# A hybrid decoder trunk in fp32 on one core: which engine takes the low halves of the GLU weights, and which the convolution taps

## The chip, the cores and the metric

The kernel runs on one core of a Trainium2 chip. The metric is the device time of one execution in microseconds (us); lower is better.

## The reference

```python
def conv_recurrent_mixer(hn, w_in, conv_a_w, ...):
    u = hn @ w_in
    a_val, a_gate, xr, gr = jnp.split(u, [D_A, 2 * D_A, 2 * D_A + D_B], axis=-1)
    ya = a_val * jax.nn.sigmoid(a_gate)
    ya = causal_depthwise_conv(ya, conv_a_w, conv_a_b)      # 31 taps per channel
    ya = jax.nn.silu(layer_norm(ya, ln_a_g, ln_a_b))
    xr = causal_depthwise_conv(xr, conv_b_w, conv_b_b)      # 4 taps
    yb = rg_lru(xr, ...) * jax.nn.gelu(gr)
    return jnp.concatenate([ya, yb], axis=-1) @ w_out
```

Layer 0 runs this mixer, layer 1 a stick-breaking attention; each layer then has a squared-ReLU MLP and a gated per-layer embedding. D is 2048, the sequence has 256 tokens, D_A and D_B are 1024, all values are float32. The change touches the part of layer 0 between the recurrent projections and the output projection, some 100 to 250 us into the execution.

## The kernel before, in words

**Chunks.** All weights arrive as 812 chunks of 512 rows by 256 columns (512 KB), numbered in the order of use. A chunk m goes through four stations. SyncE loads it into `raw[m % 4]`, once `lo` of chunk m-4 is there. ScalarE rounds it to fp32r, the `hi` half, into `spl[m % 8]` (once TensorE has used chunk m-8). VectorE (`split`, L1337) or GpSimd (L463) subtracts `hi` from `raw`: the `lo` half. TensorE then multiplies hi*hi, hi*lo and lo*hi (`three`, L533 to L535: 24 matmuls of 256 columns for a chunk). The tuple `SUMMED` names the chunks whose `lo` is GpSimd's; both other users look it up, so each chunk has one owner.

**The stretch.** Chunks 34 to 65 are the GLU projections of four pairs of channel tiles, eight chunks to a pair (`C_GLU` = 34). Chunks 66 to 81 (`C_OUTB`) are half of the output projection. While TensorE uses chunk m, VectorE's program is at the `lo` of chunk m+8. Up to the first convolution VectorE also has the recurrent group's work: `short_conv` (L1583, L1585), the decay, the scan, and the `glu_gate` of pair 0 (L1723, L1736).

**The convolution of a pair** has 31 taps for each of two tiles. Of the first tile, `FIRSTS` = 19 taps run on VectorE (L1778, L1781) and 12 as products on ScalarE, summed by GpSimd (L470, L474). Of the second, `TAPS_PE[pair]` taps run on TensorE as fp32 matmuls with a diagonal matrix that ScalarE makes (L803, L1174), the others on VectorE (L1788, L1793). VectorE's `conv(pair, q)` puts an eighth of its taps ahead of each `split`; `seconds(n)` says how many taps of the second tile are done after n of the first. TensorE does its taps of a pair in three or four lots between chunks; the first lot waits for `glu_ready` of that pair, which VectorE's L1736 gives. `conv_end(pair)` joins the parts and adds the tiles into `nacc` (L1818). After pair 3, TensorE's `ln_mean(1)` (L818) waits for that, in the middle of the group that uses chunks 74 and 75.

Every engine works through its program in order, with semaphores between them.

Of the kernel before, what the change touches and what calls it, by code (L numbers as in the profile page):

```python
# [55 lines left out]
G_GLU, C_GLU = 8, 34  # L56
G_OUTB, C_OUTB = 16, 66
G_PLE0, C_PLE0 = 24, 82
# [9 lines left out]

H_MLP0, H_GATE0, H_OUT1, H_MLP1, H_GATE1 = 0, 32, 40, 48, 80
NDG = 22  # L70
TAPS_PE = (14, 14, 14, 12)
TAPS_POOL = 12
FIRSTS = CA - TAPS_POOL

# [25 lines left out]
OUT_PIECES = ((0, 2), (2, 6), (6, 11), (11, 16))  # L100


SUMMED = tuple(k for k in range(C_GLU + 17, C_PLE0, 2) if (k - C_GLU - 17) % 8 < 6)


def cuts(m):
# [22 lines left out]
def trunk(nc, xT, pT, par, w_in, w_rg_a, w_rg_x, w_out, w_qkv, w_o, w_up, w_down, w_proj, w_gate, outT):  # L129
    with ExitStack() as ctx:  # L130
# [308 lines left out]
        @block.gpsimd  # L439
        def _(pool):  # L440
            pool.memset(onesD[:, :], 1.0 / D)
            pool.memset(onesA[:, :], 1.0 / DA)
            pool.memset(epsb[:, :], EPS)
            pool.memset(y2[:, 0:P], 1.0)
            pool.memset(glu[:, :, 0:PAD_A], 0.0)
            pool.memset(xrp[:, :, 0:PAD_B], 0.0)
            pool.memset(tl[:, 0, 0:P], -1.0)
            pool.memset(tl[:, 1, 0:P], 1.0).then_inc(consts_ready, 1)
            pool.wait_ge(consts_ready, 1)

            pool.affine_select(out=tl[:, 0, P:2 * P], in_=tl[:, 0, 0:P], compare_op=ALU.is_ge, fill=0.0, base=0,
                               pattern=[[-1, P]], channel_multiplier=1)
            pool.affine_select(out=ident[:, :], in_=y2[:, 0:P], compare_op=ALU.is_equal, fill=0.0, base=0,
                               pattern=[[-1, P]], channel_multiplier=1)

            pool.affine_select(out=mask[:, :], in_=tl[:, 1, 0:P], compare_op=ALU.is_gt, fill=0.0, base=0,
                               pattern=[[1, P]], channel_multiplier=-1).then_inc(consts_ready, 1)


            for n, m in enumerate(SUMMED):  # L460
                pool.wait_ge(hi_ready, m + 1)
                w = spl[:, m % NSPL, :, :, :]
                pool.tensor_tensor(w[:, :, 1, :], raw[:, m % NRAW, :, :], w[:, :, 0, :].bitcast(F32),  # L463
                                   ALU.subtract).then_inc(lo_summed[m % NSPL], 16)
                pair, turn = n // 3, n % 3
                for k in range(max(1, turn * TAPS_POOL // 3), (turn + 1) * TAPS_POOL // 3):
                    pool.wait_ge(prod_ready, pair * TAPS_POOL + k + 1)
                    o = y[:, 2 * pair, :]
                    if k == 1:
                        pool.tensor_tensor(o, prod[:, prod_slot(pair, 0), :], prod[:, prod_slot(pair, 1), :],  # L470
                                           ALU.add).then_inc(pool_step, 1)
                    else:
                        pool.wait_ge(pool_step, pool_adds(pair, k - 1))
                        pool.tensor_tensor(o, o, prod[:, prod_slot(pair, k), :], ALU.add).then_inc(pool_step, 1)  # L474


            pool.wait_ge(att_tiles, 8)
            pool.memset(tl[:, 0, 0:P], 1.0).then_inc(ident_ready, 1)
            pool.wait_ge(ident_ready, 1)
            pool.affine_select(out=tl[:, 1, 0:P], in_=tl[:, 0, 0:P], compare_op=ALU.is_equal, fill=0.0, base=0,  # L480
                               pattern=[[-1, P]], channel_multiplier=1).then_inc(ident_ready, 1)
# [849 lines left out]
        def _(dve):  # L1331
# [428 lines left out]
            def conv(pair, q):  # L1760
# [14 lines left out]
                for n in range(q * FIRSTS // 8, (q + 1) * FIRSTS // 8):  # L1775
                    x, w = glu[:, 2 * pair, n:n + T], par_col(pair * (2 * CA) + (CONV_A_W + n))
                    if n == 0:
                        r = dve.tensor_scalar(first, x, w, par_col(pair * 2 + CONV_A_B), ALU.mult, ALU.add)  # L1778
                    else:
                        dve.wait_ge(conv_step, base + n + seconds(n - 1))  # L1780
                        r = dve.scalar_tensor_tensor(out=first, in0=x, scalar=w, in1=first, op0=ALU.mult, op1=ALU.add)  # L1781
                    r.then_inc(conv_step, 1)
                    if seconds(n + 1) > seconds(n):
                        j = seconds(n)
                        x = glu[:, 2 * pair + 1, on_pe + j:on_pe + j + T]
                        w = par_col(pair * (2 * CA) + (CONV_A_W + CA + on_pe + j))
                        if j == 0:
                            r = dve.tensor_scalar(second, x, w, par_col(pair * 2 + (1 + CONV_A_B)), ALU.mult, ALU.add)  # L1788
                        else:

                            n0 = max(k for k in range(n) if seconds(k + 1) > seconds(k))
                            dve.wait_ge(conv_step, base + n0 + 1 + j)
                            r = dve.scalar_tensor_tensor(out=second, in0=x, scalar=w, in1=second,  # L1793
                                                         op0=ALU.mult, op1=ALU.add)
                        r.then_inc(conv_step, 1)
# [224 lines left out]
```

## Time and profile before

| | us |
|---|---|
| median of 3 runs | 2348.19 (2347.66 to 2349.77) |
| the profiled execution | 2347.8 |
| its span, first to last record | 2346.1 |
| TensorE busy within the span | 2324.9 |
| VectorE, ScalarE, GpSimd busy | 1534.6, 1252.6, 77.1 |

The span is what the profile sees; 1.7 us lie around it. Busy time of TensorE is close to the span, so the question at each place is whether TensorE has to wait there, and for whom.

### The profile page before, as it was taken

What the parts mean: (1) busy time and instruction counts of PE and PEld (TensorE: products, weight loads), DVE (VectorE), ACT (ScalarE), POOL (GpSimd) and SP (SyncE); (2) the same over time, 40 slices, a digit from 0 to 9 for tenths busy, and PEclk for the clock granted to TensorE, in tenths of its full rate; (3) what the DMA queues carried; (4) which work ended last, traced back from release to release, by engine and by line L of the source; (5) the groups of instructions that cost most, each with busy time, mean ns of one, the idle gap of its engine ahead of it and who ended that gap; (6) DMA issues with size and microseconds to landing.
All of it is one profiled execution on the core that took longest, in us unless ns stands there. A gap on an engine that the chain in (4) does not pass through costs nothing.

```text
span 2346.1 us, 39851 instructions
## 1 busy us (share of the span) xinstructions
PE 2324.9 (99%) x13964; PEld 2078.5 (89%) x13964; DVE 1534.6 (65%) x1848; ACT 1252.6 (53%) x1616; POOL 77.1 (3%) x73
## 2 busy tenths in 40 slices
PE   8999999999999999999999999999999999999998
PEld 7999998888888888888888888888888888888887
DVE  8899776556556555668676666765555555556666
ACT  6876655445445435556666666555444444445454
POOL 0046100000000000000000000000000000000000
PEclk9999999999999999999999999999999999999999
DMA  8555465655655665665555555565556556556553
GB/s 254 181 181 161 154 206 172 195 179 190 194 189 182 191 199 179 188 205 174 186 179 157 176 170 177 180 190 179 189 196 188 180 194 198 179 184 202 186 166 122
DMA packets 432334, 431.24 MB, mean 184 GB/s; under 512 B 13312, under 2 KB 430208, under 8 KB 432256
## 3 DMA queue, kind: packets, MB, share of 16 engines
q1 hardware_dynamic: 431968, 429.97, 58.1%
q8 instruction: 49, 0.80, 0.1%
q10 hardware_dynamic: 288, 0.23, 0.0%
q14 instruction: 29, 0.24, 0.0%
HBM read 428.05 MB, written 2.10 MB: 183 GB/s over the span
## 4 chain that ended last, share of the span: by engine, by line
PE 97%; DVE 1%; ACT 1%; DMA 1%; issue 0%; DVEq 0%; ACTq 0%; SPq 0%
PE ps L492 54%; PE ps L498 28%; PE ps L533 3%; PE ps L534 3%; PE ps L535 3%; PE ps L490 2%; PE ps L497 1%; PE O L803 1%; DVE spl L1337 1%; DMA raw<-in_w_o 0%; PE O L654 0%; PE Z L628 0%; ACT spl L861 0%; PE Z L637 0%; PE ps L707 0%
## 5 line engine op out<-in xcount | busy, mean ns | idle before, releaser
L1337 DVE TENSOR_TENSOR spl<-raw,spl 128x1024 fp32r<-128x1024 f32 x797 | 938.6, 1222 | 579.5 <-ACT spl L861 572.2
L861 ACT ACTIVATE spl<-raw 128x1024 fp32r<-128x1024 f32 (+1 forms) x811 | 817.3, 1054 | 686.5 <-PE ps L498 593.7
L492 PE MATMUL ps<-XA,spl 128*128 128x512 f32 x2816 | 705.0, 392 | 7.3 <-DVE spl L1545 6.7
L492 PE MATMUL ps<-XB,spl 128*128 128x512 f32 x2784 | 711.5, 392 | 0.0
L492 PEld LDWEIGHTS ps<-XA,spl 128*128 128x128 f32 x2816 | 505.1, 189 | 91.5 <-issue 7.4
L492 PEld LDWEIGHTS ps<-XB,spl 128*128 128x128 f32 x2784 | 491.4, 188 | 75.6
L498 PEld LDWEIGHTS ps<-XB,spl 128*128 128x128 f32 x2784 | 394.5, 191 | 39.0
L498 PEld LDWEIGHTS ps<-XA,spl 128*128 128x128 f32 x2816 | 387.3, 191 | 31.4
L498 PE MATMUL ps<-XB,spl 128*128 128x256 f32 x2784 | 402.6, 281 | 0.0
L498 PE MATMUL ps<-XA,spl 128*128 128x256 f32 x2816 | 393.8, 282 | 0.0
L1373 DVE TENSOR_TENSOR tv<-cross,ps 128x512 f32<-128x512 f32 x181 | 123.2, 681 | 13.2 <-ACT cross L861 13.0
L941 ACT ACTIVATE tv<-tv 128x512 f32<-128x512 f32 x64 | 40.5, 633 | 168.8 <-DVE tv L1428 168.8
L861 ACT ACTIVATE cross<-ps 128x512 f32<-128x512 f32 (+1 forms) x184 | 106.4, 578 | 12.1 <-PE ps L498 11.9
L490 PE MATMUL ps<-spl,XB 128*128 128x512 f32 x256 | 80.7, 397 | 0.0
L533 PE MATMUL ps<-XB,spl 128*128 128x256 f32 x256 | 73.9, 289 | 0.0
L533 PE MATMUL ps<-XA,spl 128*128 128x256 f32 x256 | 73.7, 288 | 0.0
L534 PE MATMUL ps<-XA,spl 128*128 128x256 f32 x256 | 72.4, 283 | 0.0
L535 PE MATMUL ps<-XA,spl 128*128 128x256 f32 x256 | 72.4, 283 | 0.0
L534 PE MATMUL ps<-XB,spl 128*128 128x256 f32 x256 | 72.4, 283 | 0.0
L535 PE MATMUL ps<-XB,spl 128*128 128x256 f32 x256 | 72.4, 283 | 0.0
L1415 DVE TENSOR_TENSOR h<-h,tv 128x512 f32 (+1 forms) x87 | 60.3, 693 | 12.6 <-DVE tv L1373 11.3
L914 ACT ACTIVATE tv<-h 128x512 f32 (+1 forms) x47 | 29.7, 631 | 60.5 <-DVE h L1415 58.7
(207 smaller groups left out, 1531.6 us busy)
## 6 DMA issues: line engine op xcount, KB each, us to landing
raw<-in_w_up SPq DMA_DIRECT2D x256, 512.0 KB, 4.8
raw<-in_w_down SPq DMA_DIRECT2D x256, 512.0 KB, 5.2
raw<-in_w_qkv SPq DMA_DIRECT2D x96, 512.0 KB, 4.4
raw<-in_w_gate SPq DMA_DIRECT2D x64, 512.0 KB, 4.6
raw<-in_w_in SPq DMA_DIRECT2D x63, 512.0 KB, 4.7
raw<-in_w_out SPq DMA_DIRECT2D x32, 512.0 KB, 3.6
raw<-in_w_o SPq DMA_DIRECT2D x32, 512.0 KB, 4.8
raw<-in_w_proj SPq DMA_DIRECT2D x8, 512.0 KB, 4.1
```

What stands on the lines that cost most here:

```text
L490: pe.matmul(ps[:, b + o, :], x[:, kt, 0, c], w[:, q, :, :], start=start, stop=False)
L492: pe.matmul(ps[:, b + o, :], w[:, q, 0, c], x[:, kt, :, :], start=start, stop=False)
L498: return pe.matmul(ps[:, b + o, 0:256], w[:, q, 1, c], x[:, kt, 0, :], start=False, stop=stop)
L533: pe.matmul(out, w[0], x[0], start=start, stop=False, skip_group_check=True)
L534: pe.matmul(out, w[0], x[1], start=False, stop=False, skip_group_check=True)
L535: return pe.matmul(out, w[1], x[0], start=False, stop=stop, skip_group_check=True)
L861: return act.activation(out, in_, ACT.Copy, scale=scale)
L914: act.activation(tv[:, :, :], h[:, bass.ds(t0, 2), :], ACT.Square).then_inc(sq_ready, 1)
L941: act.activation(tv[:, :, :], tv[:, :, :], ACT.Square).then_inc(up_sq, 1)
L1337: dve.tensor_tensor(s[:, :, 1, :], raw[:, m % NRAW, :, :], s[:, :, 0, :].bitcast(F32), ALU.subtract).then_inc(lo_ready, 1)
L1373: dve.tensor_tensor(tv[:, :, :] if out is None else out, cross[:, :, :], ps[:, b:b + 2, 0:256], ALU.add).then_inc(sum_ready, 1)
L1415: dve.tensor_tensor(ht, ht, tv[:, :, :], ALU.add).then_inc(res_ready, 1)
```

## The change

Three things, in one step. `SUMMED` grows from 12 to 23 chunks: the even chunks 36 to 48 (`EARLY`, seven) and all odd ones from 51 to 81 (sixteen) in place of the twelve odd ones that left out 57, 65, 73 and 81. `TAPS_PE` falls from (14, 14, 14, 12) to (9, 9, 9, 8), so that 19 taps go from TensorE to VectorE, which now has 22 or 23 taps of the second tile among 19 of the first. GpSimd's sums of products are spread over four chunks of a pair, three at a time, in place of three chunks with four each.

```diff
-TAPS_PE = (14, 14, 14, 12)
+TAPS_PE = (9, 9, 9, 8)
...
-SUMMED = tuple(k for k in range(C_GLU + 17, C_PLE0, 2) if (k - C_GLU - 17) % 8 < 6)
+EARLY = tuple(range(C_GLU + 2, C_GLU + 16, 2))
+SUMMED = EARLY + tuple(range(C_GLU + 17, C_PLE0, 2))
...
-                pair, turn = n // 3, n % 3
-                for k in range(max(1, turn * TAPS_POOL // 3), (turn + 1) * TAPS_POOL // 3):
+                if m in EARLY:
+                    continue
+                pair, turn = (n - len(EARLY)) // 4, (n - len(EARLY)) % 4
+                for k in range(max(1, turn * TAPS_POOL // 4), (turn + 1) * TAPS_POOL // 4):
...
-                    if seconds(n + 1) > seconds(n):
-                        j = seconds(n)
+                    for j in range(seconds(n), seconds(n + 1)):
...
-                            n0 = max(k for k in range(n) if seconds(k + 1) > seconds(k))
+                            n0 = max(k for k in range(n + 1) if seconds(k) <= j - 1)
```

VectorE ahead of the first convolution, from the scan of the recurrent group's second half (L1704) to its first tap (L1778). Rows `spl<-raw,spl` are `lo` halves of chunks; `rg`, `dec`, `mlt`, `pp` are the recurrent group's tiles. Before:

```order
L1337 TENSOR_TENSOR spl<-raw,spl 128x4x256 x2
L1698 TENSOR_TENSOR rg<-rg,mlt 128x4x256
L1704 SCALAR_TENSOR_TENSOR rg<-dec,rg 128x256 x4
L1337 TENSOR_TENSOR spl<-raw,spl 128x4x256 x2
L1710 TENSOR_TENSOR pp<-rg,pp 128x1024
L1337 TENSOR_TENSOR spl<-raw,spl 128x4x256 x2
L1723 TENSOR_TENSOR tv<-ps,rB 128x512
L1337 TENSOR_TENSOR spl<-raw,spl 128x4x256
L1736 TENSOR_TENSOR glu<-glu,tv 128x2x256
L1337 TENSOR_TENSOR spl<-raw,spl 128x4x256 x2
```

and now:

```order
L1340 TENSOR_TENSOR spl<-raw,spl 128x4x256
L1701 TENSOR_TENSOR rg<-rg,mlt 128x4x256
L1707 SCALAR_TENSOR_TENSOR rg<-dec,rg 128x256 x4
L1340 TENSOR_TENSOR spl<-raw,spl 128x4x256
L1713 TENSOR_TENSOR pp<-rg,pp 128x1024
L1340 TENSOR_TENSOR spl<-raw,spl 128x4x256
L1726 TENSOR_TENSOR tv<-ps,rB 128x512
L1340 TENSOR_TENSOR spl<-raw,spl 128x4x256
L1739 TENSOR_TENSOR glu<-glu,tv 128x2x256
L1340 TENSOR_TENSOR spl<-raw,spl 128x4x256
```

Every pair of `lo` halves has become one; the other one stands on GpSimd.

GpSimd, from its constants to the end of its work for pair 0; `rest` holds the products. Before:

```order
L456 AFFINE_SELECT mask<-tl 128x128
L463 TENSOR_TENSOR spl<-raw,spl 128x4x256
L470 TENSOR_TENSOR y<-rest 128x256
L474 TENSOR_TENSOR y<-y,rest 128x256 x2
L463 TENSOR_TENSOR spl<-raw,spl 128x4x256
L474 TENSOR_TENSOR y<-y,rest 128x256 x4
L463 TENSOR_TENSOR spl<-raw,spl 128x4x256
L474 TENSOR_TENSOR y<-y,rest 128x256 x4
```

and now:

```order
L457 AFFINE_SELECT mask<-tl 128x128
L464 TENSOR_TENSOR spl<-raw,spl 128x4x256 x8
L473 TENSOR_TENSOR y<-rest 128x256
L477 TENSOR_TENSOR y<-y,rest 128x256
L464 TENSOR_TENSOR spl<-raw,spl 128x4x256
L477 TENSOR_TENSOR y<-y,rest 128x256 x3
L464 TENSOR_TENSOR spl<-raw,spl 128x4x256
L477 TENSOR_TENSOR y<-y,rest 128x256 x3
L464 TENSOR_TENSOR spl<-raw,spl 128x4x256
L477 TENSOR_TENSOR y<-y,rest 128x256 x3
```

Seven `lo` halves (chunks 36 to 48) now stand ahead of that of chunk 51, and a pair has four of them with three sums each at most.

VectorE in the convolution of pair 0, from the eighth tap of the first tile to the next `lo` half of the program. Before:

```order
L1781 SCALAR_TENSOR_TENSOR Z<-glu,params,Z 128x256 x2
L1793 SCALAR_TENSOR_TENSOR Z<-glu,params,Z 128x256
L1337 TENSOR_TENSOR spl<-raw,spl 128x4x256
```

and now:

```order
L1784 SCALAR_TENSOR_TENSOR Z<-glu,params,Z 128x256
L1795 SCALAR_TENSOR_TENSOR Z<-glu,params,Z 128x256
L1784 SCALAR_TENSOR_TENSOR Z<-glu,params,Z 128x256
L1795 SCALAR_TENSOR_TENSOR Z<-glu,params,Z 128x256
L1340 TENSOR_TENSOR spl<-raw,spl 128x4x256
```

Where two taps of the first tile (L1781) stood in a row there is now one of the second tile between them; at three other places of a pair (four in pair 3) two taps of the second tile (L1795) stand in a row.

## Rows read from the trace of the kernel before

**Rows 1.** The page: busy time of each engine over the span.

```profile
PE 2324.9 (99%) x13964; PEld 2078.5 (89%) x13964; DVE 1534.6 (65%) x1848; ACT 1252.6 (53%) x1616; POOL 77.1 (3%) x73
```

**Rows 2.** Busy time by stretch: length, then PE, PEld, DVE, ACT, POOL.

```profile
95.00:140.00 45.00, 45.00 (x356) 43.93 (x355) 42.09 (x49) 38.15 (x54) 0.00 (x0) 1.00 0.50 155
140.00:248.00 108.00, 106.31 (x802) 103.20 (x800) 103.11 (x201) 70.72 (x138) 74.56 (x56) 1.00 0.54 165
```

**Rows 3.** Waits of TensorE, 60 to 300 us: total, times, longest.

```profile
PE Z L818 <- DVE nacc L1818: 1.7, 1, 1.7
```

**Rows 4.** Timeline of TensorE: start, duration; lots of four and of three taps.

```profile
145.13 1.89 PE L803 MATMUL O<-glu,dg 128*128 128x256 f32 x8
146.67 0.47 PE L533 MATMUL ps<-XA,spl 128*128 128x256 f32 x1
...
220.82 1.46 PE L803 MATMUL O<-glu,dg 128*128 128x256 f32 x6
221.93 0.47 PE L533 MATMUL ps<-XB,spl 128*128 128x256 f32 x1
```

**Rows 5.** Timeline of VectorE in the convolution of pair 0: taps and a lo half.

```profile
149.94 1.01 DVE L1781 SCALAR_TENSOR_TENSOR Z<-glu,params,Z 128x256 f32<-128x256 f32 x2
150.86 0.48 DVE L1793 SCALAR_TENSOR_TENSOR Z<-glu,params,Z 128x256 f32<-128x256 f32 x1
151.25 1.24 DVE L1337 TENSOR_TENSOR spl<-raw,spl 128x1024 fp32r<-128x1024 f32 x1
152.41 0.47 DVE L1781 SCALAR_TENSOR_TENSOR Z<-glu,params,Z 128x256 f32<-128x256 f32 x1
```

**Rows 6.** VectorE: the gate of pair 3, a wait, and the sum that TensorE awaits.

```profile
216.95 0.69 DVE L1736 TENSOR_TENSOR glu<-glu,tv 128x512 f32<-128x512 f32 x1 [0.77 <-ACT tv L1128]
...
226.34 1.23 DVE L1337 TENSOR_TENSOR spl<-raw,spl 128x1024 fp32r<-128x1024 f32 x1 [1.17 <-ACT spl L861]
...
247.03 0.89 DVE L1818 TENSOR_TENSOR nacc<-nacc,y 128x256 f32<-128x256 f32 x2
```

**Rows 7.** TensorE at the mean of the layer norm.

```profile
247.97 0.70 PE L818 MATMUL Z<-nacc,onesA 128*128 128x256 f32 x2 [1.69 <-DVE nacc L1818]
```

**Rows 8.** Timelines of GpSimd and of VectorE where both work from SBUF alone.

```profile
154.79 2.40 POOL L463 TENSOR_TENSOR spl<-raw,spl 128x1024 fp32r<-128x1024 f32 x1
...
229.33 2.42 POOL L463 TENSOR_TENSOR spl<-raw,spl 128x1024 fp32r<-128x1024 f32 x1 [0.30 <-ACT spl L861]
...
156.33 1.95 DVE L1337 TENSOR_TENSOR spl<-raw,spl 128x1024 fp32r<-128x1024 f32 x1
...
230.89 2.02 DVE L1818 TENSOR_TENSOR nacc<-nacc,y 128x256 f32<-128x256 f32 x2
```

**Rows 9.** GpSimd's first lo half of pair 1, and VectorE's beside it.

```profile
168.82 2.90 POOL L463 TENSOR_TENSOR spl<-raw,spl 128x1024 fp32r<-128x1024 f32 x1 [5.48 <-ACT spl L861]
...
168.24 1.21 DVE L1337 TENSOR_TENSOR spl<-raw,spl 128x1024 fp32r<-128x1024 f32 x1
```

**Rows 10.** ScalarE, VectorE and TensorE ahead of the first convolution.

```profile
97.97 1.99 ACT L861 ACTIVATE spl<-raw 128x1024 fp32r<-128x1024 f32 x2
...
97.72 2.46 DVE L1585 SCALAR_TENSOR_TENSOR pp<-xrp,params,pp 128x256 f32<-128x256 f32 x6
...
102.49 0.69 DVE L1366 TENSOR_TENSOR XB<-pp,XB 128x512 fp32r<-128x512 f32 x1
...
122.17 2.35 DVE L1337 TENSOR_TENSOR spl<-raw,spl 128x1024 fp32r<-128x1024 f32 x2
...
128.05 2.33 DVE L1337 TENSOR_TENSOR spl<-raw,spl 128x1024 fp32r<-128x1024 f32 x2
...
138.90 1.22 DVE L1337 TENSOR_TENSOR spl<-raw,spl 128x1024 fp32r<-128x1024 f32 x1 [0.65 <-ACT spl L861]
...
103.37 1.60 PE L770 MATMUL O<-XB,wrg 128*128 128x256 f32 x12
104.81 0.28 PE L533 MATMUL ps<-XA,spl 128*128 128x256 f32 x1
```

## What the change will do: prediction

> **What bounds the kernel now.** I read the page's busy times first: TensorE is busy 2324.9 of 2346.1 us, VectorE 1534.6 [rows 1]. That looks like a kernel in which every matmul taken away is time won. So I then asked for the table by stretch around the convolution. Between 140 and 248 us VectorE is busy 103.11 of 108.00 us, and between 95 and 140 us 42.09 of 45.00 [rows 2]. This is the one part in which two engines are full. The waits of TensorE between 60 and 300 us have one line only: 1.7 us for the sum `nacc`, at the mean of the layer norm [rows 3, 7]. There VectorE ends last already: its sum is done at 247.03 + 0.89 = 247.92 and TensorE, idle for 1.69 us, starts at 247.97. TensorE works through its program in order, so all after this point hangs on VectorE's end. A change that takes work from TensorE ahead of it and gives work to VectorE wins nothing unless VectorE ends earlier. I therefore sum VectorE's program up to 247.92, not TensorE's.
>
> **TensorE's part.** A lot of four taps holds TensorE from 145.13 to 146.67 (1.54 us), a lot of three from 220.82 to 221.93 (1.11 us) [rows 4]. One tap is the difference, 0.43 us; the number of lots stays. 19 taps are 8.2 us, of which 15 (6.5 us) lie ahead of pair 3's first lot. ScalarE makes 19 diagonal matrices fewer; it is off the path in the convolution (70.72 of 108.00 us busy [rows 2]) and I cost that at nothing.
>
> **VectorE's part in the convolution.** A tap starts at 150.86 and the next instruction at 151.25: 0.39 us. A `lo` half starts at 151.25 and the next at 152.41: 1.16 us. Two taps of one tile in a row take from 149.94 to 150.86, 0.92 us, 0.14 more than two apart [rows 5], since the second needs the first's result. The change adds 19 x 0.39 = 7.4 us. It makes 3 + 3 + 3 + 4 = 13 new places with two taps in a row and removes six (two in each of pairs 0 to 2): 7 x 0.14 = 1.0 us. It removes the `lo` halves of chunks 57, 65, 73 and 81: 4 x 1.16 = 4.6 us. Together **+3.8 us** to the sum; to the gate of pair 3 it is 15 x 0.39 + 3 x 0.14 - 3 x 1.16 = +2.8 us. VectorE's wait of 1.17 us for a `hi` half at 226.34 [rows 6] goes, for TensorE frees the buffers earlier as seen from a later VectorE: **-1.2 us**.
>
> **The seven early chunks.** On VectorE each costs 1.16 us, so the plain reckoning gives back 8.1 us. Here the trace speaks against it. GpSimd's `lo` half takes 2.4 us, and it doesn't run beside VectorE. GpSimd's at 154.79 ended at 157.19. VectorE's, started at 156.33, took 1.95 us, to 158.28: 1.1 us, its usual time, after GpSimd's end. GpSimd's at 229.33 ended at 231.75; two additions from `nacc` and `y`, started at 230.89, took 2.02 us, to 232.91, against 0.89 elsewhere [rows 6, 8]. It holds the other way too: VectorE's from 168.24 to 169.45 makes GpSimd's, issued at 168.82, last 2.90 us [rows 9]. So two instructions that each read two SBUF operands exclude one another for their whole length. Taps on VectorE read one operand from PSUM (`Z`) and go on at 0.39 us; that is why this costs little in the convolution now. But ahead of it nearly all of VectorE's work is of the exposed kind: the small convolution's sums, the decay, the scan, the `lo` halves, and it is busy 42.09 of 45.00 us [rows 2]. There each handed-over chunk takes 1.16 us from VectorE and puts 2.41 us of exclusion on it: 1.25 us the worse. `hi` of chunk 36, the first of two from 97.97 to 99.96, is there at about 99.0, while VectorE is in six such sums (97.72 to 100.18) [rows 10], and the next ones meet the scans and the other products likewise. Only the seventh (chunk 48) falls where VectorE waits for ScalarE anyway (0.65 us ahead of 138.90 [rows 10]). I take 6 x 1.25 = **+7.5 us** for VectorE's start into the convolution. The ends: -8.1 if nothing collides and VectorE can use all of it, 7 x 2.41 = +16.9 less 8.1 = +8.8 if all seven collide in full.
>
> The Trainium skill, "SBUF — State Buffer", section "SBUF: two separate sides", says that VectorE and GpSimd share one port pair as an exclusive lock: a VectorE instruction with two SBUF inputs and a GpSimd one that reads SBUF block each other, whichever starts first, for the whole instruction. By this rule the early part costs; by two engines that merely run side by side it would gain. The trace agrees with the rule in both directions (1.95 and 2.90 us above).
>
> Two places pass the delay on to TensorE at once. Its gate matmuls at 103.37 need VectorE's result of 102.49 + 0.69 = 103.18: 0.2 us of slack. And chunks follow one another from 104.81 with (145.13 - 104.81) / 14 = 2.88 us each [rows 4, 10], so chunk 43 is due at 104.81 + 9 x 2.88 = 130.7, while its `lo` is ready at 128.05 + 1.16 = 129.2: 1.5 us of slack. Four of the collisions come ahead of it, 5.0 us, so TensorE should stand some 3.5 us there. Chunk 41 (the first of two at 122.17, due at 125.0) is as tight.
>
> **GpSimd and its sums.** Four more `lo` halves in the convolution are 4 x 2.41 us more of exclusion, of which VectorE meets a part; the two collisions of rows 8 cost it 0.7 and 1.1 us. I take **+1.0 us**, between 0 and 5.0. The last three sums of pair 3 now follow chunk 81's `lo`, but `hi` of it comes with TensorE's progress and VectorE is later still, so nothing waits for them.
>
> **The sum.** VectorE's `nacc`: 247.92 + 7.5 + 3.8 - 1.2 + 1.0 = 259.0, that is **+11.1 us**. TensorE would reach pair 3's first lot at 220.82 - 6.5 + 3.5 = 217.8, the gate is ready at 216.95 + 0.69 + 7.5 + 2.8 = 227.9: a wait of 10 us, new. From there it needs 246.28 - 220.82 - 4 x 0.43 = 23.7 us to the mean, so it is there at 251.7 and waits 7 us. What follows moves with it. 2347.8 + 11.1 = 2358.9 for the profiled execution; the median stands 0.4 us above that one, so 2359.
>
> **The rivals.**
>
> A: the early collisions fall into VectorE's idle time and cost nothing, but it can't use the freed 8.1 us either, since it then waits for ScalarE (38.15 of 45.00 us busy, and already what ended the wait at 138.90). It starts the convolution 1.5 us earlier, an estimate from the 2.9 us that it idles in that stretch. -1.5 + 3.8 - 1.2 = +1.1: 2349.3, no measurable change, though 19 taps left TensorE; it would stand idle for them. For it: GpSimd is empty there. Against it: VectorE's 42.09 of 45.00.
>
> B: VectorE gains all 8.1 us: -8.1 + 3.8 - 1.2 = -5.5, so 2342.7, **faster**. TensorE, 8.2 us less loaded, reaches the mean at 238.1 and doesn't limit this. It decides from the point at which the early `lo` halves cost VectorE less than 0.2 of their 1.16 us and ScalarE follows. The exclusion and ScalarE's part both speak against it.
>
> C: as forecast, but in the convolution each of the four added `lo` halves also puts 1.25 us on VectorE: 5.0 in place of 1.0, with the early ones at their end of +8.8: 2347.8 + 8.8 + 3.8 - 1.2 + 5.0 = 2364.2.
>
> **How the numbers follow.** A difference of 0.2% (4.7 us) is about what a measurement of this kernel tells from none. Forecast 0.62, A 0.22, B 0.08, C 0.08. Slower is forecast and C, 0.70; same is A, 0.22; faster is B, 0.08. The range 2348 to 2365 takes in C and most of A and leaves out B.
>
> **What would show it.** Right: VectorE's early two-operand steps last 2 to 3 us in place of 1.2, its first tap starts near 147.5 in place of 138.90 + 1.16 = 140.1, TensorE waits for `lo` of chunks 41 or 43, for the gate of pair 3 (some 10 us) and at the mean (some 7). Wrong: a first tap at or ahead of 140 with early steps of 1.2 us, which is A or B; or TensorE waits only at the mean.

## The result, and the profile after

| us | before | changed |
|---|---|---|
| median, six runs each, same chip | 2348.98 (2347.66 to 2351.10) | 2369.36 (2364.94 to 2370.24) |
| the profiled execution | 2347.8 | 2367.35 |
| its span | 2346.1 | 2365.6 |
| first tap of the convolution (VectorE) | 140.04 | 147.68 |
| `nacc` done (VectorE) | 247.92 | 265.87 |
| TensorE starts the mean | 247.97 | 265.92 |

The changed kernel is slower: ratio 1.0083, interval 1.0072 to 1.0094, or 20.4 us. 2359 was forecast and the range ended at 2365. So the direction was right, and the time lies outside the range by 4 us. The page first, for the changed kernel (share of the span, instructions):

```profile
PE 2322.6 (98%) x13926; PEld 2074.7 (88%) x13926; DVE 1550.4 (66%) x1856; ACT 1248.7 (53%) x1597; POOL 105.4 (4%) x84
```

TensorE is busy 2.3 us less than in [rows 1], for a span that is 19.5 us longer. (It sheds 8.2 us of taps; part of that comes back as the same matmuls at a lower clock, below.) So the time went into waiting. The table by stretch, as [rows 2] (length, then PE, PEld, DVE, ACT, POOL; the third figure from the end is the granted clock):

```profile
95.00:140.00 45.00, 40.71 (x303) 39.13 (x302) 42.58 (x38) 32.05 (x46) 15.95 (x6) 0.96 0.35 113
140.00:248.00 108.00, 93.42 (x707) 89.39 (x706) 102.05 (x184) 63.54 (x112) 74.49 (x50) 0.97 0.50 158
```

VectorE is as full as before and gets less done: 38 instructions instead of 49 in the first stretch (six of the eleven are `lo` halves handed over), 184 instead of 201 in the second. TensorE, which before idled only the 1.7 us of [rows 3] here, now idles 4.3 us in the first and 14.6 in the second. Its waits between 60 and 330 us (total, times, longest), where [rows 3] had one line:

```profile
PE O L806 <- DVE glu L1739: 9.0, 1, 9.0
PE O L806 <- ACT dg L1177: 5.4, 3, 2.9
PE Z L821 <- DVE nacc L1820: 4.6, 1, 4.6
PE O L773 <- DVE XB L1369: 2.6, 1, 2.6
PE ps L536 <- DVE spl L1340: 1.7, 2, 1.0
```

The 5.4 us for `dg`, ScalarE's diagonal matrices, are 1.3 us in pair 1 and 1.2 and 2.9 us in pair 2, all ahead of the gate of pair 3. ScalarE makes these matrices behind its own wait for VectorE's `tv` (9.3 us ahead of 205.02), so this wait too goes back to VectorE.

**Ahead of the convolution.** Timeline of VectorE in the changed kernel (start, duration; the steps of [rows 10] and those that grew):

```profile
97.62 4.61 DVE L1588 SCALAR_TENSOR_TENSOR pp<-xrp,params,pp 128x256 f32<-128x256 f32 x6
...
110.45 3.44 DVE L1681 TENSOR_TENSOR rg<-rg,pp 128x1024 f32<-128x1024 f32 x1
...
116.19 4.61 DVE L1707 TENSOR_TENSOR_SCAN rg<-dec,rg 128x256 f32<-128x256 f32 x4
...
123.69 3.22 DVE L1687 TENSOR_TENSOR rg<-dec 128x1024 f32<-128x1024 f32 x1
...
130.55 4.60 DVE L1707 TENSOR_TENSOR_SCAN rg<-dec,rg 128x256 f32<-128x256 f32 x4
...
136.20 3.41 DVE L1713 TENSOR_TENSOR pp<-rg,pp 128x1024 f32<-128x1024 f32 x1
...
145.85 1.90 DVE L1340 TENSOR_TENSOR spl<-raw,spl 128x1024 fp32r<-128x1024 f32 x1 [1.95 <-ACT spl L864]
147.68 0.53 DVE L1781 TENSOR_SCALAR Z<-glu,params 128x256 f32<-128x256 f32 x1
```

and of GpSimd beside it, two of its seven early `lo` halves:

```profile
99.06 2.49 POOL L464 TENSOR_TENSOR spl<-raw,spl 128x1024 fp32r<-128x1024 f32 x1 [96.32 <-ACT spl L864]
110.18 2.62 POOL L464 TENSOR_TENSOR spl<-raw,spl 128x1024 fp32r<-128x1024 f32 x1 [8.63 <-ACT spl L864]
```

Six of VectorE's groups lost 2.0 to 2.2 us each (4.61 for the 2.46 of [rows 10], 3.4 for 1.2), and a seventh, the `lo` half at 145.85, 0.7 us. Each loss stands over one `lo` half of GpSimd. The one at 110.18 shows how: it ends at 112.80, and VectorE's sum, started at 110.45, ends 1.09 us later, after its own length.

**In the convolution.** Timeline of VectorE in the changed kernel: the steps longer than [rows 5] would have them, and the end:

```profile
154.92 2.93 DVE L1340 TENSOR_TENSOR spl<-raw,spl 128x1024 fp32r<-128x1024 f32 x1
...
161.62 2.00 DVE L1340 TENSOR_TENSOR spl<-raw,spl 128x1024 fp32r<-128x1024 f32 x1
...
167.99 1.94 DVE L1340 TENSOR_TENSOR spl<-raw,spl 128x1024 fp32r<-128x1024 f32 x1
...
185.11 2.95 DVE L1340 TENSOR_TENSOR spl<-raw,spl 128x1024 fp32r<-128x1024 f32 x1
...
191.50 1.56 DVE L1820 TENSOR_TENSOR nacc<-y 128x256 f32<-128x256 f32 x1
...
213.82 2.93 DVE L1340 TENSOR_TENSOR spl<-raw,spl 128x1024 fp32r<-128x1024 f32 x1
...
220.19 2.39 DVE L1820 TENSOR_TENSOR nacc<-nacc,y 128x256 f32<-128x256 f32 x2
...
264.08 0.42 DVE L1809 TENSOR_TENSOR y<-y,Z 128x256 f32<-128x256 f32 x1 [0.77 <-POOL y L477]
...
264.99 0.88 DVE L1820 TENSOR_TENSOR nacc<-nacc,y 128x256 f32<-128x256 f32 x2
```

The `lo` half behind the eleventh tap takes 2.93, 2.95 and 2.93 us in pairs 0, 1 and 2. GpSimd's beside the first of them:

```profile
153.65 0.74 POOL L477 TENSOR_TENSOR y<-y,rest 128x256 f32<-128x256 f32 x1
154.35 2.42 POOL L464 TENSOR_TENSOR spl<-raw,spl 128x1024 fp32r<-128x1024 f32 x1
```

It starts 0.57 us ahead of VectorE's, which then waits for its end at 156.77. The other two start at 184.57 and 213.27, both 0.54 to 0.55 ahead. Three times the same meeting, so it comes from the order of the two programs, not from chance. The table gives the same reading for each pair, as the time that VectorE's steps took beyond their usual 1.22 (a `lo` half), 0.48 (`nacc`) and 0.89 (two of it):

| pair | first tap to next first tap: before, after | more by taps and `lo` halves | beyond usual, before | beyond usual, after | sum | measured |
|---|---|---|---|---|---|---|
| 0 | 26.77, 30.17 | 0.93 | 0.7 | 1.7 + 0.8 + 0.7 | 3.4 | 3.40 |
| 1 | 25.02, 28.71 | 0.93 | 0.1 | 1.7 + 1.1 | 3.6 | 3.69 |
| 2 | 25.92, 29.64 | 0.93 | 0.5 + 0.1 | 1.7 + 1.5 + 0.2 | 3.7 | 3.72 |
| 3, to `nacc` | 30.17, 29.67 | 0.96 | 1.1, waits 1.4 | 0.5, wait 0.8 | -0.2 | -0.50 |

0.93 is the prediction's own arithmetic for one pair, 5 x 0.39 + 0.14 - 1.16. With 7.64 ahead of it the four pairs make 17.95 us, which is the whole shift of `nacc`.

**At the mean and behind it.** TensorE in the changed kernel, for [rows 7]:

```profile
265.92 0.82 PE L821 MATMUL Z<-nacc,onesA 128*128 128x256 f32 x2 [4.56 <-DVE nacc L1820]
266.27 0.68 PE L536 MATMUL ps<-XB,spl 128*128 128x256 f32 x1
266.75 0.41 PE L537 MATMUL ps<-XB,spl 128*128 128x256 f32 x1
...
269.89 0.28 PE L537 MATMUL ps<-XB,spl 128*128 128x256 f32 x1
```

and TensorE's stretches there (length, busy, count, granted clock, DMA share, GB/s):

```profile
265.00:270.00 5.00, 4.08 (x19) 0.66 0.36 111
270.00:275.00 5.00, 5.00 (x44) 1.00 0.01 5
```

The matmuls behind the wait last 0.41 us and follow one another by 0.21; from 269.9 on they last 0.28 and follow by 0.12. That is the clock's lower level, 1.2 GHz, for some 3.5 us, and then 2.4 again. Before, behind a wait of 1.69 us, they last 0.28 from the second on and the clock stays 1.00. From the start of the mean to the end of the span it is 2098.1 us before and 2099.7 now, 1.5 us more. That this is the low level's price is shown by the next pair of matmuls of `ln_mean`: they start 10.7 us behind the first now and 9.2 before. (The whole rest of the span alone wouldn't show it: in e6, e7, e11 and e12, all at clock 1.00 behind the mean, it is 2098.8 to 2099.1 us.) 17.95 + 1.5 is the 19.5 of the span.

### The profile page after: what moved, and what is told of

It is laid out like the page before. It is cut to its first block, busy times and chain, and to the rows that moved or that the text cites. A ratio compares the mean times of both kernels' runs of the same rounds, so it can differ in the third digit from the quotient of the medians.

```text
span 2365.6 us, 39786 instructions
## 1 busy us (share of the span) xinstructions
PE 2322.6 (98%) x13926; PEld 2074.7 (88%) x13926; DVE 1550.4 (66%) x1856; ACT 1248.7 (53%) x1597; POOL 105.4 (4%) x84
## 4 chain that ended last, share of the span: by engine, by line
PE 88%; DVE 8%; ACT 2%; DMA 1%; issue 1%; POOL 0%; SPq 0%; DVEq 0%; ACTq 0%; POOLq 0%
PE ps L495 51%; PE ps L501 27%; PE ps L493 2%; DVE spl L1340 2%; PE ps L536 1%; PE ps L537 1%; PE ps L538 1%; PE ps L500 1%; DVE Z L1795 1%; DMA raw<-in_w_in 1%; DVE Z L1784 1%; ACT spl L864 1%; DVE pp L1588 0%; PE O L657 0%; PE Z L631 0%
## 5 line engine op out<-in xcount | busy, mean ns | idle before, releaser
L864 ACT ACTIVATE cross<-ps 128x512 f32<-128x512 f32 (+1 forms) x184 | 106.8, 580 | 11.6 <-PE ps L501 11.6
L464 POOL TENSOR_TENSOR spl<-raw,spl 128x1024 fp32r<-128x1024 f32 x23 | 62.6, 2722 | 153.5 <-ACT spl L864 153.5
```

The costliest lines, as they stand in the source:

```text
L864: return act.activation(out, in_, ACT.Copy, scale=scale)
```

## The experiments

Medians are of 4 to 11 runs, against 9 to 21 of the kernel before on the same chip. Lines of the code are those of each kernel. Two cautions: experiments on different chips have different medians of the kernel before (2348.45 to 2349.60), and the profiled executions stand apart already at VectorE's instruction near 95 us, whose code is the same in all, from 1.2 us earlier (e8) to 2.9 later (e5) than in the kernel before. Lengths of pairs are free of both.

| | what | us | before | ratio, interval |
|---|---|---|---|---|
| e1 | early chunks alone | 2355.85 | 2349.20 | 1.0030 (1.0018 to 1.0043) |
| e2 | 19 taps alone | 2359.85 | 2349.20 | 1.0047 (1.0031 to 1.0064) |
| e3 | the change without early chunks | 2362.05 | 2349.20 | 1.0055 (1.0039 to 1.0072) |
| e4 | the change, sums in three lots | 2367.19 | 2349.20 | 1.0075 (1.0058 to 1.0092) |
| e5 | before, seven extra reads on GpSimd | 2362.82 | 2348.45 | 1.0059 (1.0042 to 1.0075) |
| e6 | before, 21 fills on GpSimd | 2349.16 | 2348.45 | 1.0000 (0.9990 to 1.0010) |
| e7 | before, the four `lo` halves alone | 2347.75 | 2348.45 | 0.9997 (0.9987 to 1.0006) |
| e8 | e3, GpSimd's `lo` in turn | 2355.64 | 2348.45 | 1.0031 (1.0018 to 1.0044) |
| e9 | e8 with 51 taps on TensorE | 2352.52 | 2349.60 | 1.0013 (1.0004 to 1.0022) |
| e10 | the change, all in turn | 2360.28 | 2349.60 | 1.0046 (1.0031 to 1.0062) |
| e11 | e9, sums in three lots | 2346.47 | 2348.68 | 0.9993 (0.9984 to 1.0002) |
| e12 | e11 with 54 taps on TensorE | 2348.38 | 2348.68 | 0.9996 (0.9987 to 1.0005) |

**The parts of the change.** The theory at this point: the early chunks cost some 7 us by exclusion, and the rest comes from GpSimd's second `lo` half of a pair standing right ahead of VectorE's. Why it stands there has two candidates: one sum less ahead of it, or the convolution's late start, which shifts VectorE against ScalarE and GpSimd.

e1, the early chunks alone:

```diff
--- before
-SUMMED = tuple(k for k in range(C_GLU + 17, C_PLE0, 2) if (k - C_GLU - 17) % 8 < 6)
+EARLY = tuple(range(C_GLU + 2, C_GLU + 16, 2))
+SUMMED = EARLY + tuple(k for k in range(C_GLU + 17, C_PLE0, 2) if (k - C_GLU - 17) % 8 < 6)
...
-                pair, turn = n // 3, n % 3
+                if m in EARLY:
+                    continue
+                pair, turn = (n - len(EARLY)) // 3, (n - len(EARLY)) % 3
```

> The kernel before with one part of the change: GpSimd takes the lo halves of the seven even chunks 36 to 48; taps and sums are as before. Theory (two engines that each read two SBUF operands exclude one another, so each such chunk costs VectorE 2.4 us in place of 1.16): VectorE's first tap starts 7 to 8 us later (near 147.7 in place of 140.0), TensorE waits ahead of 140 us for XB and for the lo halves of chunks 41 and 43, and the whole is 6 to 8 us slower, near 2355. Rival (handing over is a gain, and the taps made the changed kernel slow): first tap at or ahead of 140, 2347 to 2349.

It is 6.7 us slower. The first tap stands at 147.53, 7.5 later than before, with the same long steps as above. The pairs then take 26.79, 25.06 and 25.90 us, as before. So a late start by itself makes no new collision in the convolution of the kernel before. The shift at the mean is less, 6.0 us (253.95), since in pair 3 VectorE no longer waits for the `hi` half: the prediction's term of -1.2.

e2, the taps alone:

```diff
--- before
-TAPS_PE = (14, 14, 14, 12)
+TAPS_PE = (9, 9, 9, 8)
...
-                    if seconds(n + 1) > seconds(n):
-                        j = seconds(n)
+                    for j in range(seconds(n), seconds(n + 1)):
...
```

> The kernel before with another part of the change: 35 taps on TensorE, 19 more on VectorE; GpSimd has its twelve chunks as before. Theory (VectorE's end sets the mean of the layer norm): the sum nacc comes 8.4 - 1.4 = 7.0 us later, TensorE waits some 9 us for the gate of pair 3 and some 5 at the mean, and the whole is 7 to 9 us slower, near 2356.5. Rival (TensorE's work counts): 8 us faster, 2341.

10.7 us slower in the median, 3.4 more than expected; the profiled execution (2357.7) lies 2 us below that median. TensorE starts the mean 8.1 us later than before, at 256.11, after waits of 11.0 us for the gate of pair 3 and 5.3 at the mean. Taking 8.2 us from TensorE alone makes the kernel slower by more than that, since all of it goes to the engine that ends last. From 255 to 260 us the granted clock is 0.53, the second part of the price. Pairs 0 to 2 take 85.57 us together for 77.71 before; 6.27 of the 7.86 more are the taps themselves (three times 5 x 0.39 + 0.14), so 1.6 us are longer meetings, though GpSimd's program is untouched. The `lo` half behind the eleventh tap lasts 1.43 to 1.44 us here: the added taps alone don't make the meeting of 2.93.

e3, the change without its early chunks:

```diff
--- changed
-EARLY = tuple(range(C_GLU + 2, C_GLU + 16, 2))
+EARLY = ()
```

> The changed kernel without the seven early chunks on GpSimd. Theory: VectorE's first tap is back at 140.0, the convolution keeps its length, with VectorE's lo half behind the eleventh tap of each of pairs 0 to 2 lasting 2.9 us for GpSimd's beside it; 7.6 us and some clock less than the changed kernel: 2359 to 2362, so 10 to 13 us slower than before. Rival (the long lo halves in the convolution come from the late start): these last 1.2 us, and it is 3 to 5 us slower than before, near 2353.

12.9 us slower than before, so with e1's 6.7 the parts add up to 19.5 of 20.4 us. Its timelines, VectorE's second `lo` half of pairs 0 and 1, and GpSimd's beside the first:

```profile
148.31 3.20 DVE L1340 TENSOR_TENSOR spl<-raw,spl 128x1024 fp32r<-128x1024 f32 x1
...
178.83 2.94 DVE L1340 TENSOR_TENSOR spl<-raw,spl 128x1024 fp32r<-128x1024 f32 x1
...
148.02 2.41 POOL L464 TENSOR_TENSOR spl<-raw,spl 128x1024 fp32r<-128x1024 f32 x1 [0.23 <-ACT spl L864]
```

The first tap is at 141.06 here, 6.6 us earlier than in the changed kernel (8.2 when both are counted from the instruction near 95 us), and the long `lo` halves are all there (the third: 2.94 at 207.53). The late start falls as their cause.

e4, the change with GpSimd's sums back in three lots (3, 4 and 4, none behind the fourth `lo`):

```diff
--- changed
-                for k in range(max(1, turn * TAPS_POOL // 4), (turn + 1) * TAPS_POOL // 4):
+                for k in range(max(1, turn * TAPS_POOL // 3), (turn + 1) * TAPS_POOL // 3 if turn < 3 else 0):
```

> The changed kernel with GpSimd's sums of a pair behind its first three lo halves (three, four and four of them, as in the kernel before) and none behind the fourth. Theory (a matter of phase: with one sum less ahead of it, GpSimd's second lo half of a pair begins just ahead of VectorE's, which then waits for nearly all of it): VectorE's lo half behind the eleventh tap goes first and lasts 1.2 to 1.4 us in place of 2.9, 1.5 us less in each of pairs 0 to 2, also no wait for the last sums (0.8): 4 to 6 us faster than the changed kernel, near 2364. Rival (the amount of GpSimd's work counts, which is the same): 2369.

Only 2.2 us faster than the change where 4 to 6 were expected, and the intervals of the two ratios (1.0058 to 1.0092 and 1.0072 to 1.0094) overlap, so that a gain isn't clear of the noise. VectorE's `lo` halves of e4 behind the eleventh tap of pair 0 and behind a later one of pair 1, and GpSimd's beside that:

```profile
155.60 1.66 DVE L1340 TENSOR_TENSOR spl<-raw,spl 128x1024 fp32r<-128x1024 f32 x1
...
190.10 3.45 DVE L1340 TENSOR_TENSOR spl<-raw,spl 128x1024 fp32r<-128x1024 f32 x1
...
190.06 2.41 POOL L464 TENSOR_TENSOR spl<-raw,spl 128x1024 fp32r<-128x1024 f32 x1
```

The second `lo` halves do shrink, to 1.66, 1.44 and 1.45 us: the number of sums ahead sets that meeting, as the theory says. But others appear in its place (3.45 at 190.10, 2.31 at 197.91, 2.52 at 220.58). Pair 0 gets shorter by 2.7 us, pair 1 longer by 0.9. The sums move the meetings about; they don't remove them. The three pairs take 86.50 us, for 88.52 in the change and 77.71 before. Of the 8.0 us that meetings add to them in the change 6.0 are still there with the sums in their old order; the new order accounts for the 2.0 between.

**What excludes.** Rival to the exclusion by reads: any instruction on GpSimd, or the changed order of VectorE's program, makes VectorE slow. e5 leaves VectorE's program as before and adds seven subtractions of two SBUF operands on GpSimd, unrelated to the result, each once the `hi` half of one of those seven chunks is there:

```diff
--- before
+            for e, m in enumerate(range(C_GLU + 2, C_GLU + 16, 2)):
+                pool.wait_ge(hi_ready, m + 1)
...
+                o = rest[:, 0:1024].rearrange("p (b n) -> p b n", n=P)
+                pool.tensor_tensor(o, bcast(onesD[:, :], 8), bcast(onesA[:, :], 8), ALU.subtract).then_inc(extra_done, 1)
...
```

In both runs ScalarE also waits for these instructions before it writes its first product of pair 0 into the same buffer. e6 has three fills of the same 128x1024 tile there instead:

```diff
--- e5
-                pool.tensor_tensor(o, bcast(onesD[:, :], 8), bcast(onesA[:, :], 8), ALU.subtract).then_inc(extra_done, 1)
+                for k in range(3):
...
+                    pool.memset(rest[:, 0:1024], 0.0).then_inc(extra_done, 1)
```

> The kernel before, with seven instructions more on GpSimd, one after each hi half of the even chunks 36 to 48: a subtraction of 128x1024 elements with two SBUF operands that nothing else uses (onesD and onesA into a free tile). VectorE does all its lo halves itself, as before, so nothing is handed over and no lo half comes from a slower engine. Theory (mutual exclusion of instructions with two SBUF operands): each puts some 2.4 us on VectorE; its first tap comes 12 to 17 us later than 140.0, and the kernel is 12 to 17 us slower, near 2363. Rival (the early hand-over cost time because GpSimd's lo halves are late for the buffers or for TensorE): VectorE is as before, 2348 to 2350.

> As the run with extra reads, but with three fills of 128x1024 elements (no SBUF operand to read) in place of each subtraction. Theory in its stronger form (only GpSimd instructions that read SBUF exclude VectorE's): no change, 2348 to 2350, and VectorE's instructions last as before. If any GpSimd instruction excludes VectorE's: slower by about the fills' own time, 5 to 15 us.

e5 is 14.4 us slower. Its timelines of VectorE and GpSimd:

```profile
104.23 3.29 DVE L1699 SCALAR_TENSOR_TENSOR mlt<-rg,mlt 128x1024 f32<-128x1024 f32 x1
...
113.35 3.44 DVE L1346 TENSOR_TENSOR spl<-raw,spl 128x1024 fp32r<-128x1024 f32 x1
...
101.98 4.46 POOL L466 TENSOR_TENSOR rest<-onesD,onesA 128x1024 f32<-128x1024 f32 x1 [99.24 <-ACT spl L868]
113.01 2.70 POOL L466 TENSOR_TENSOR rest<-onesD,onesA 128x1024 f32<-128x1024 f32 x1 [6.57 <-ACT spl L868]
```

The first shows both directions. GpSimd's is issued at 101.98, while VectorE goes from step to step without a gap (its next ones start at 102.18, 102.58 and 102.97), and finishes at 106.44. That is its own 2.4 us counted from about 104.0, near the end of the last of these steps (104.19); VectorE's next, from 104.23, then waits for it and lasts 3.29. The first tap is at 156.12; with 2.88 us taken off, by which this profiled execution was already later near 95 us, that is 13.2 us later than before, of at most 7 x 2.41 = 16.9.

e6 is the same as before within 0.1%. VectorE's six sums and GpSimd's fills beside them:

```profile
98.70 2.46 DVE L1594 SCALAR_TENSOR_TENSOR pp<-xrp,params,pp 128x256 f32<-128x256 f32 x6
...
100.05 3.00 POOL L466 MEMSET rest<- 128x1024 f32 x3 [97.31 <-ACT spl L868]
```

2.46 us, to the hundredth what [rows 10] has, with GpSimd at work for the second half of it. The 21 fills are 21 us of GpSimd's time, more than e5's seven subtractions take by themselves (7 x 2.4). So instructions of GpSimd that only write don't exclude VectorE's; those that read two operands do. The rival falls. The Trainium skill, "SBUF — State Buffer", section "SBUF: two separate sides", names just these pairs, a VectorE instruction with two SBUF inputs against a GpSimd one that reads SBUF, and the traces agree with it, for `scalar_tensor_tensor` and the scan too.

**Are the four added `lo` halves the cause?** e7 gives them to GpSimd in the kernel before, with its sums left as they were:

```diff
--- before
-SUMMED = tuple(k for k in range(C_GLU + 17, C_PLE0, 2) if (k - C_GLU - 17) % 8 < 6)
+SUMMED = tuple(range(C_GLU + 17, C_PLE0, 2))
...
-                pair, turn = n // 3, n % 3
+                pair, turn = n // 4, n % 4
+                if turn == 3:
+                    continue
```

> The kernel before with the third part of the change alone: GpSimd also takes the lo halves of chunks 57, 65, 73 and 81 (the fourth of each pair), its sums stay behind the first three, taps as before. Theory: VectorE saves up to 4.6 us, but ends last at the mean of the layer norm by only 1.7 us, and GpSimd's fourth lo half pushes its other ones to other moments: 1.7 us faster to 3 us slower, 2346.5 to 2351, no clear change. Rival (each GpSimd lo half costs VectorE what it costs early, 1.25 us): 5 us slower, 2354.

No change that can be measured. The pairs take 26.32, 28.73 and 24.77 us: pair 1 holds three meetings, two of which are

```profile
166.84 3.38 DVE L1339 TENSOR_TENSOR spl<-raw,spl 128x1024 fp32r<-128x1024 f32 x1
...
179.46 2.43 DVE L1820 TENSOR_TENSOR nacc<-y 128x256 f32<-128x256 f32 x1
```

and pairs 0 and 2 less. Together the three pairs take 79.82 us for 77.71 before, although VectorE has handed over 3 x 1.16 = 3.5 us of them: meetings take 5.6 us more than before, 1.9 for each added `lo` half. In the whole that is paid for by the four times 1.16 us and by shorter waits in pair 3: TensorE starts the mean at 246.24, 1.7 us earlier than before (0.6 of which this execution had already near 95 us). So the added `lo` halves are not free. With the 1.6 us of e2 their 5.6 make 7.2 of the 8.0 us of the change. Whether it is their number, or where they fall, the next runs ask.

**Taking the meetings away.** If it is where they fall, one wait should do what the order of the sums couldn't. e8 is e3 with a wait on GpSimd: it starts the `lo` of an odd chunk m only when VectorE has done its own of the chunk before. So GpSimd always comes right behind one, while VectorE is in its taps, which read PSUM.

```diff
--- e3
                 pool.wait_ge(hi_ready, m + 1)
+                pool.wait_ge(lo_ready, cuts(m))
```

> The changed kernel without the early chunks (as the run without early), and with one wait more: GpSimd starts the lo half of chunk m only when VectorE's lo halves of all chunks below m are done, so that it falls on VectorE's taps, which read PSUM. Theory (collisions are a matter of phase): VectorE's lo halves all last 1.2 to 1.3 us, a pair takes some 2 us less, and the kernel is 5 to 8 us faster than without the wait, near 2355. Rival (what slows VectorE is the amount of GpSimd's work, or PSUM taps are slowed too): no change against 2362.

6.4 us faster than e3 in the medians (5.7 when each is taken against the kernel before on its own chip), by nothing but a wait. VectorE's second `lo` half of pair 0 in e8, then its subtraction into `XB`, a step of 128x2048 that reads SBUF alone, and GpSimd's fourth `lo` beside this:

```profile
146.02 1.22 DVE L1341 TENSOR_TENSOR spl<-raw,spl 128x1024 fp32r<-128x1024 f32 x1
...
158.04 2.82 DVE L1370 TENSOR_TENSOR XB<-pp,XB 128x2048 fp32r<-128x2048 f32 x1
...
158.67 4.46 POOL L465 TENSOR_TENSOR spl<-raw,spl 128x1024 fp32r<-128x1024 f32 x1
```

1.22 us where e3 has 3.20. The exclusion is still there, but GpSimd comes second and bears it (4.46 for 2.40), and it has time. The pairs take 27.47, 27.41 and 28.13 us, against 30.51, 28.70 and 29.65 in e3. That is 2.5 us of meetings more than before for the same number of `lo` halves, where the change has 8.0. So the number sets what can be lost, and where they fall how much of it is.

e10 has the same wait in the changed kernel, early chunks included:

```diff
--- changed
                 pool.wait_ge(hi_ready, m + 1)
+                pool.wait_ge(lo_ready, cuts(m))
```

> The changed kernel whole, with GpSimd's lo halves in turn behind VectorE's, the early ones too. Theory: the convolution takes some 7 us less, as in the run in turn without the early chunks; ahead of it only the first early chunk (36) moves to a moment at which VectorE waits anyway, which saves some 2 of the 7.6 us, for the others VectorE has no taps to run beside them: 9 to 10 us faster than the changed kernel, near 2360, and still slower than the run in turn without them by some 5. Rival (turns cure the early chunks too): 2355 to 2356.

9.1 us faster than the change. The first tap is at 145.19, 2.5 us earlier (3.6 counted from the instruction near 95 us), and pairs 0 to 2 take 5.6 us less together. Ahead of the convolution the wait helps less: there VectorE's next instructions read SBUF as well, and there is no gap for GpSimd (scans of 4.60 and 4.51 us, a `lo` half of 3.42 at 134.24).

**A version that beats both?** e9 is e8 with only three taps moved, 51 on TensorE:

```diff
--- e8
-TAPS_PE = (9, 9, 9, 8)
+TAPS_PE = (13, 13, 13, 12)
```

> A version that by the theory should beat the kernel before: all sixteen odd chunks from 51 to 81 on GpSimd, each in turn behind VectorE's (as in the run in turn), none of the early ones, and 51 taps on TensorE (13, 13, 13, 12). VectorE's sum then comes at 247.9 - 4.6 + 3 x 0.39 = 244.5 plus what collisions are left, TensorE would be at the mean at 246.3 - 3 x 0.43 = 245.0. Theory: the wait at the mean is gone or under 1 us, and the kernel is 1 to 3 us faster than before, 2346 to 2347.5. Rival (GpSimd's fourth lo half costs as much as it frees): no change, 2348.5.

A miss by 5 us. Pairs 0 to 2 are short, 25.55, 25.37 and 26.29, but at the end of pair 3 stand, of VectorE and of GpSimd:

```profile
247.05 0.42 DVE L1810 TENSOR_TENSOR y<-y,Z 128x256 f32<-128x256 f32 x1 [3.19 <-POOL y L478]
...
242.19 2.40 POOL L465 TENSOR_TENSOR spl<-raw,spl 128x1024 fp32r<-128x1024 f32 x1 [1.16 <-ACT spl L865]
244.55 2.46 POOL L478 TENSOR_TENSOR y<-y,rest 128x256 f32<-128x256 f32 x3
```

GpSimd's last three sums stand behind chunk 81's `lo`, which needs a `hi` that comes at TensorE's pace. VectorE, now early, waits 3.19 us for them, TensorE 3.83 for VectorE, and then from 250 to 255 us it has a clock of 0.54. In the change the same wait is the 0.77 us of 264.08. e11 puts these sums ahead, in three lots as in e4:

```diff
--- e9
-                for k in range(max(1, turn * TAPS_POOL // 4), (turn + 1) * TAPS_POOL // 4):
+                for k in range(max(1, turn * TAPS_POOL // 3), (turn + 1) * TAPS_POOL // 3 if turn < 3 else 0):
```

> As the run in turn with 51 taps, but GpSimd's sums of a pair stand behind its first three lo halves, so that those of pair 3 don't wait for chunk 81. That run had VectorE wait 3.2 us for them, and TensorE stood 3.8 us at the mean and then ran at half clock. Theory: the wait for the sums is gone, VectorE's sum comes near 245.7 and TensorE, there at 245.1, waits under 1 us at full clock: 1 to 3 us faster than the kernel before, 2346 to 2347.5. Rival (four sums behind a lo half put GpSimd behind and the collisions return): 2349 to 2352.

TensorE at the mean in e11:

```profile
246.46 0.70 PE L822 MATMUL Z<-nacc,onesA 128*128 128x256 f32 x2 [0.55 <-DVE nacc L1821]
```

The wait is 0.55 us and the clock 1.00 behind it. 2346.47 is 6.1 us below e9 (5.1 against each chip's own kernel before) and 2.2 below the kernel before, but the interval of that last ratio reaches 1.0002: a gain over the kernel before isn't shown. e12 takes the last three taps back as well:

```diff
--- e11
-TAPS_PE = (13, 13, 13, 12)
+TAPS_PE = (14, 14, 14, 12)
```

> The same with all 54 taps on TensorE, as before: the kernel before plus four lo halves on GpSimd, each in turn behind VectorE's. Theory: VectorE's sum comes at 243 to 245, TensorE at 246.3 doesn't wait at the mean: 1.7 us faster than before, 2346.5 to 2347.5, and 0 to 1 us slower than the run with 51 taps. Rival: as above.

No change against the kernel before, and 0.9 us above the end of what was expected. It is e7 with the wait and the same sums: pairs 0 to 2 take 76.50 us for e7's 79.82, but VectorE has now time to spare in pair 3 and waits 2.28 us for ScalarE's `hi` half at 228.54. TensorE waits 0.55 us at the mean in both, so that what VectorE gains doesn't reach the whole.

## Why the prediction was right in sign and short in size

**What bounds the kernel: right.** The sum was made along VectorE's program to `nacc`, and the time moved with that: 17.95 us there, 19.5 in the span. TensorE gave up 19 taps and waited for 9.0 us at the gate of pair 3 (10 forecast) and 4.6 at the mean (7 forecast). That the first of these came so close is luck: the gate was ready at 236.1 for 227.9, 8.2 us late, and TensorE was there at 227.2 for 217.8, 9.4 late, among others by the 5.4 us of waits for `dg`, which the forecast cost at nothing. They don't move the end, since TensorE waits for VectorE behind them. e2 shows the bound in pure form.

**The early chunks: right, the size in part by luck.** First tap at 147.68, forecast 147.5; +7.64 against +7.5, and e1 alone gives 6.7 us in the median. It was made of 6 x 1.25; the trace has six losses of 2.0 to 2.2 us and one of 0.7, less the seven times 1.16 handed over, which is 5.5, and 2.2 us more of waits for ScalarE, which no term had. e5 and e6 show that it is the reading that excludes. TensorE stood 4.3 us in that part, 3.5 forecast. Rivals A and B, in which the early chunks cost nothing or gained, fall with it.

**Taps, rows of two and `lo` halves: right.** In each of pairs 0 to 2 the +0.93 us of this arithmetic and the long steps add up to the measured length within 0.1 us.

**The wait for `hi` and pair 3: right.** -0.2 in the forecast's terms, -0.50 measured.

**GpSimd in the convolution: the term that failed.** "I take **+1.0 us**, between 0 and 5.0" measured 8.0 us in pairs 0 to 2 (3.2 + 2.8 + 3.4 beyond the usual lengths, less 0.7 + 0.1 + 0.6 before), and 7.4 with the meetings of pair 3 (0.5 for 1.1). The mechanism was the right one, the size wrong. There was no working behind 1.0: four meetings at the 0.7 and 1.1 us of [rows 8] are already 2.8 to 4.4. The runs give three parts. The added `lo` halves alone bring 5.6 us (e7, 1.9 for each of the three in these pairs); a meeting can cost VectorE up to 2.2 us (3.45 for 1.22 in e4), where 1.25, the end of rival C, was the net price of a handed-over chunk. The taps alone bring 1.6 (e2), by shifting VectorE's program against GpSimd's, which no term had. And the one sum less ahead of GpSimd's second `lo` half put it 0.55 us before VectorE's own in each of these pairs; with the old sums the three pairs are 2.0 us shorter (e4). The parts don't add up exactly: 5.6 and 1.6 are 7.2 by themselves, and e4, which has both, has 6.0. That order stands ahead of the prediction; it was read as "three sums with each" and not laid beside VectorE's times. C was nearest in kind and still 5 us low.

**"Nothing waits for them": wrong by 0.8 us here**, and by 3.2 in e9. The last sums of pair 3 stand behind chunk 81's `lo`; VectorE did come to wait for them.

**TensorE's clock: a term left out.** "What follows moves with it" took the rest of the span as a constant. After the wait of 4.56 us it is 1.5 us longer, at the lower level of the clock.

The account: 11.1 forecast, + 7.0 by the meetings, - 0.1 by the early part and pair 3 together, + 1.5 by the clock, give 19.5, the difference of the two profiled executions being 19.55. The median of the changed kernel lies 2.0 us above its profiled execution; I have no row for that.

What stays open: in which way ScalarE's `hi` halves and these meetings drive one another from pair to pair (e4 moved them in a way that I hadn't expected), and why e2's median lies 3.4 us above what was expected of it; its trace accounts for 1.1 (8.1 at the mean for 7.0) and the clock.

## What to carry to other kernels

Where two engines exclude one another for whole instructions, don't price a further such instruction by the mean of those that are there: nine of them cost 1.4 us together in pairs 0 to 2 before, three more cost 5.6 (e7). Lay the two programs side by side in time and see which of the two comes second at each meeting, since that one pays; a small step more or less ahead can make the same meeting fall in every turn of a loop. A wait that lets the idler engine begin just behind the busy engine's own such instruction took 6.4 us off without any work being moved (e8), where shuffling its work gave 2.2, not clear of the noise (e4). And work taken from an engine that is nearly always busy is worth nothing where another one ends last; ask for the one wait in its list first.

## What the runs showed of the hardware

**The exclusion is wide.** Besides plain sums it holds for VectorE's fused multiply-add (4.61 us for 2.46) and its scan (4.61 for 2.44), and 21 fills of 128x1024 on GpSimd pass without a trace in VectorE's times (e6). In a group of several VectorE steps the other engine can get in between two: of the six sums from 97.62 in the changed kernel the fifth alone is long, 2.63 us for 0.48. It doesn't always get in behind the step in progress: in e5, issued at 101.98, it came in only behind the third of the steps that followed that one without a gap. What decides this stays open.

**TensorE's clock after a wait.** What I hadn't put in the sum is that the clock doesn't only cost during a wait but behind it. `ln_mean` has a second pair of matmuls, some chunks behind the first. The time from the start of the one to that of the other, by the wait ahead of the first:

| | wait ahead, us | to the second pair, us | lowest granted clock of a 5 us stretch |
|---|---|---|---|
| e7, e11, e12 | 0.5 | 9.2 | 1.00 |
| before, e6 | 1.7 | 9.2 | 1.00 |
| e1 | 2.2 | 10.65 | 0.70 |
| e5 | 2.7 | 9.2 | 1.00 |
| e4 | 3.7 | 10.5 | 0.70 |
| e9 | 3.8 | 11.7 | 0.54 |
| changed | 4.6 | 10.7 | 0.66 |
| e3 | 4.5 | 10.65 | 0.66 |
| e8 | 4.9 | 11.1 | 0.50 |
| e2 | 5.3 | 10.8 | 0.53 |
| e10 | 6.1 | 11.6 | 0.65 |

Where the lower level came, it left 1.3 to 2.5 us of extra time behind the wait; where it didn't, none. The price doesn't grow with the wait, and the length of the wait alone doesn't decide whether it comes: behind 2.2 us it did (e1), behind 2.7 it didn't (e5). Why, these runs don't show. The same happened early in the changed kernel, where TensorE's gate matmuls at 105.28, behind a wait of 2.59 us, took 2.40 us for the 1.60 of [rows 10].
